# Byte places of the activations, and of both weight rings, in a two-layer decoder trunk

## The chip, the cores and the metric

One core of a Trainium2 chip runs the whole kernel. The metric is device time in microseconds of one launch, where lower is better. TensorE is called PE in the profile, VectorE DVE, ScalarE ACT, GpSimd POOL, and SP is the engine that issues most DMAs.

## What is computed

Sixteen learned meta tokens are put before 256 tokens of width 1024, and 272 tokens go through two layers of three sublayers each: a half-step feed-forward, a token mixer, a half-step feed-forward. Each has a norm before and one after it.

```python
h = concat([meta, x])                       # 272 x 1024, float32
for i in range(2):
    h += 0.5 * rms_norm(swiglu(rms_norm(h, g[0]), w_gate[i,0], w_up[i,0], w_down[i,0]), g[1])
    h += rms_norm(mixer(rms_norm(h, g[2])), g[3])     # i=0: retention and gated delta heads; i=1: window and stick-breaking heads
    h += 0.5 * rms_norm(swiglu(rms_norm(h, g[4]), w_gate[i,1], w_up[i,1], w_down[i,1]), g[5])
return h[16:]
# swiglu(x) = (silu(x @ w_gate) * (x @ w_up)) @ w_down, 1024 -> 2816 -> 1024
```

## The kernel before, in words

The activations lie transposed: 128 features on the partitions, eight blocks of them (`KD`, index kk) side by side, 272 tokens along a row. The weights come from memory in chunks of 128 partitions x 8 blocks x 256 columns of float32 (`RAW` = 2048 elements, 8192 bytes a partition; chunks of a down projection have 7 or 8 blocks). There are about 170 chunks, numbered n through the whole program.

*Splitting.* Each float32 value is split into a high part, rounded to the type float32r, and a low part, the rest, also float32r. A product is then three matmuls in float32r: high weights by high activations, low weights by high activations, high weights by low activations. That is `tile`: L1800, L1801, L1802, once for each of eight kk and each of the two 128-column halves of a chunk, 48 matmuls in all. In each of them the weights are the stationary operand (128x128) and the activations the moving one (272 columns, 256 where the meta tokens are no longer wanted). In the last down projection (`last_down`, L1888 to L1890) it is the other way: the weights move, 512 columns at a time, and the hidden activations are stationary. `first_tiles` (L1834, L1837, L1838), `half_tile` (L1872) and `out_half` (L2030) do the same products in other orders.

*Rings.* SP loads chunk n into slot n % 6 of `raw` (`NR` = 6). ScalarE (`hi`, L717) rounds it into slot n % 4 of `w_hi` (`NW` = 4), and VectorE (`lo`, L1179) writes the difference back over the same bytes, under the name `w_lo`. PE waits for the low part and reads both. Semaphores order the engines; `hi` and `lo` stand in each engine's program one to three chunks ahead of PE's use.

*Activations.* `u` (the sublayer's input) and `hid` (the hidden layer of a feed-forward) each have a high half and a low half. A row of them has `ROW` = 320 elements (1280 bytes) for 272 tokens, so that each kk begins at the same byte address modulo 256. Where the tokens start in a row is set by a number of bytes for each sublayer (`U_AT` for six sublayers, `HID_AT` for four feed-forwards). In "ab" the first half of the output projection reads two other buffers, `mix_hi` and `mix_lo`, whose rows are 1088 bytes. The six sublayers are, in order, ffn, ab, ffn, ffn, cd, ffn. The output projection of "cd" and the last sublayer skip the meta tokens and so begin 64 bytes later in a row.

*Places.* The address of a buffer modulo 256 follows from the assertion that `u_room` is at 64 and from the sizes: `raw` starts 49152 + 32768 + 1088 + 2176 = 85184 bytes before it, which is 192 modulo 256, so it starts at 128. All slots of `raw`, `w_lo` and `w_hi` are at 128 then, since a slot is 8192 bytes; a kk step in a chunk is 1024 bytes and the second half of its columns 512 bytes on, both nothing modulo 256. High and low `u` and `hid` are at 64, in the last feed-forward at 128 (and 192 with the skipped tokens). The scales of the norms, `gains`, sit in spare columns of `u`'s rows (elements 288 to 319), as do a few small tables of the "ab" mixer.

```python
def parts(name, rows_, where, shift):
    both = at(name, [P, 2 * rows_ * ROW], F32R, where)[:, :].rearrange("p (z k c) -> p z k c", z=2, c=ROW)
    cols = slice(shift // 4, shift // 4 + T)
    return both[:, 0, :, cols], both[:, 1, :, cols]
```

Of the kernel before, what the change touches and what calls it, by code (L numbers as in the profile page):

```python
# [22 lines left out]
F32 = mybir.dt.float32  # L23
# [5 lines left out]
P = 128  # L29
# [21 lines left out]
PLACE = 64  # L51
U_AT = (0, 0, 0, 0, 0, 64)
HID_AT = (0, 0, 0, 64)
# [99 lines left out]
def build(nc, a, c, out):  # L153
# [18 lines left out]
    with ctx:  # L172

        ring = place[0]
        raw = sb("raw", [NR, RAW])
        w_lo = at("w_lo", [P, NR, RAW], F32R, ring)
        w_hi = sb("w_hi", [NW, RAW], F32R)
        ss = sb("ss", [T])
        rstd = sb("rstd", [2, T])
        u_place = place[0]  # L180
# [28 lines left out]
        y_sq = at("y_sq", [P, 2, 2, T], F32, scratch)  # L209
        h_tok = at("h_tok", [P, 2, D], F32, place[0])  # L210
# [368 lines left out]
        def _(sp):  # L579
# [3 lines left out]
            def load(n, src, cols=CB):  # L583
# [3 lines left out]
                dst = raw[:, n % NR, 0:rows(n) * CB].rearrange("p (k c) -> p k c", c=cols)  # L587
                sp.dma_start(dst, src).then_inc(s_raw[n % NR], 16)

            for k, (kind, b, layer, f) in enumerate(subs):  # L590
                if kind == "ffn":
# [3 lines left out]
                    for j in range(NPAIR - 1):  # L595
                        if k == 0 and j == 0:
                            for k0, done in ((0, s_rawa), (KD // 2, s_raw[0])):
                                sp.dma_start(raw[:, 0, k0 * CB:(k0 + KD // 2) * CB].rearrange("p (k c) -> p k c", c=CB),
# [108 lines left out]
        def _(act):  # L707
            step = Steps(act, s_act)

            def hi(n):  # L710
# [6 lines left out]
                act.activation(w_hi[:, n % NW, 0:rows(n) * CB], raw[:, n % NR, 0:rows(n) * CB], ACT.Copy)\  # L717
# [46 lines left out]
            def pre_norm(k, kind, layer, b):  # L764
# [5 lines left out]
                for g in range(KD // 2):  # L770
                    if k == 0 and g == 2:
                        act.wait_ge(s_raw[0], 16)
                        act.activation(w_hi[:, 0, RAW // 2:RAW], raw[:, 0, RAW // 2:RAW], ACT.Copy).then_inc(s_hi, 1)
# [11 lines left out]
                if k == 0:  # L785
                    act.wait_ge(s_raw[1], 16)
                    for part, done in ((slice(0, RAW // 2), s_hia), (slice(RAW // 2, RAW), s_hi)):
                        act.activation(w_hi[:, 1, part], raw[:, 1, part], ACT.Copy).then_inc(done, 1)
# [345 lines left out]
            act.activation(w_hi[:, 0, 0:RAW // 2], raw[:, 0, 0:RAW // 2], ACT.Copy).then_inc(s_hia, 1)  # L1134
# [33 lines left out]
        def _(dve):  # L1168
# [4 lines left out]
            def lo(n):  # L1173
# [4 lines left out]
                src, dst = raw[:, n % NR, 0:rows(n) * CB], w_lo[:, n % NR, 0:rows(n) * CB]  # L1178
# [58 lines left out]
            def make_input(k, kind, layer):  # L1237
# [6 lines left out]
                for g in range(KD // 2):  # L1244
                    if k and g + 1 < KD // 2:
                        update_h(k, 2 * g + 2, 2 * g + 4)
                    if k == 0 and g == 2:
                        dve.wait_ge(s_hi, 1)
                        dve.tensor_tensor(w_lo[:, 0, RAW // 2:RAW], raw[:, 0, RAW // 2:RAW],
                                          w_hi[:, 0, RAW // 2:RAW].bitcast(F32), ALU.subtract).then_inc(s_lo, 1)  # L1250
                    input_lo(k, layer, g)
                if k == 0:
                    for part, ready, n, done in ((slice(0, RAW // 2), s_hia, 2, s_loa), (slice(RAW // 2, RAW), s_hi, 2, s_lo)):
                        dve.wait_ge(ready, n)
                        dve.tensor_tensor(w_lo[:, 1, part], raw[:, 1, part], w_hi[:, 1, part].bitcast(F32), ALU.subtract)\
# [1210 lines left out]
```

## Time and profile before

| | |
|---|---|
| median of 2 runs | 1092.18 us (1091.97 to 1092.39) |
| the profiled execution | 1091.99 us, of which the span of instructions is 1090.2 us |
| PE busy in the span | 1077.6 us, 8599 instructions |
| DVE busy | 703.7 us, 770 instructions |
| ACT busy | 545.4 us, 635 instructions |
| PE clock granted | 0.999 of full speed on the mean |
| memory traffic | 180.02 MB by DMA, mean 165 GB/s |

The page gives, for each engine, the time in which some instruction of it is under way. PE's matmuls overlap: a second one starts while the first is still in flight, so their durations add up to more than the busy time, and the distance from start to start is what the engine needs for one. Instructions of one line of the source are one group, and a group may mix shapes ("+1 forms"). A stretch of the timeline gives each instruction's start and duration; consecutive ones of one kind may be merged into one row with their count ("x2"). A window counts what overlaps it, so what was in flight at its left edge is counted too.

### The profile page before, as it was taken

Reading aid. Unit: us, or ns where it says so; the run is one execution under the profiler, and the core shown is the slowest. Engines: PE = TensorE matmul, PEld = TensorE weight load, DVE = VectorE, ACT = ScalarE, POOL = GpSimd, SP = SyncE. Lnnn points to the kernel's source line nnn. Section 1 sums busy time; section 2 is a strip of 40 time slices with the busy share of each in tenths; the row PEclk is TensorE's granted clock in tenths of the full one; section 3 lists DMA queues with packets and bytes.
Section 4 is the critical chain, followed back from the end, with each engine's and each line's share of the span. In section 5 each row is a group of like instructions: output and inputs, shape, how many; then the busy total and the mean of one; then the engine's idle time right before and its main releaser. Section 6 shows DMA issues by size and latency. Waiting matters only on the chain.

```text
span 1090.2 us, 19370 instructions
## 1 busy us (share of the span) xinstructions
PE 1077.6 (99%) x8599; PEld 1046.3 (96%) x8599; DVE 703.7 (65%) x770; ACT 545.4 (50%) x635; POOL 1.6 (0%) x13
## 2 busy tenths in 40 slices
PE   9999999999999999999999999999999999999997
PEld 8999999999999999999999999999999899999986
DVE  6755654588996777655546755654568867665552
ACT  5644343477564755343544644343575766444431
POOL 0000000000000000000000000000000000000000
PEclk9999999999999999999999999999999999999999
DMA  9666556857841455554554655555553245666451
GB/s 315 195 191 184 181 174 166 161 110 189 171 147 39 155 155 179 169 193 151 178 180 130 213 185 164 183 174 179 160 179 117 78 155 156 193 193 207 142 173 39
DMA packets 173073, 180.02 MB, mean 165 GB/s; under 512 B 7509, under 2 KB 165805, under 8 KB 172989
## 3 DMA queue, kind: packets, MB, share of 16 engines
q1 hardware_dynamic: 172668, 177.66, 54.0%
q8 instruction: 68, 1.11, 0.4%
q10 hardware_dynamic: 320, 1.11, 0.3%
q14 instruction: 17, 0.13, 0.0%
HBM read 177.05 MB, written 1.71 MB: 164 GB/s over the span
## 4 chain that ended last, share of the span: by engine, by line
PE 90%; DVE 6%; ACT 2%; issue 1%; DMA 1%; ACTq 0%; DVEq 0%
PE ps L1800 24%; PE ps L1802 23%; PE ps L1801 23%; PE ps L1905 5%; PE ps L1888 2%; PE ps L1890 2%; PE ps L1889 2%; PE ps L2030 2%; PE ps L1872 2%; PE ps L1834 1%; PE ps L1837 1%; PE ps L1838 1%; DVE hT L1228 1%; DVE w_lo L1179 1%; DVE yT L1227 1%
## 5 line engine op out<-in xcount | busy, mean ns | idle before, releaser
L1800 PE MATMUL ps<-u,w_hi 128*128 128x272 f32 (+1 forms) x1648 | 473.6, 287 | 1.2 <-DVE w_lo L1179 0.9
L1802 PE MATMUL ps<-u,w_hi 128*128 128x272 f32 (+1 forms) x1648 | 470.0, 285 | 0.0
L1801 PE MATMUL ps<-u,w_lo 128*128 128x272 f32 (+1 forms) x1648 | 469.7, 285 | 0.0
L1179 DVE TENSOR_TENSOR w_lo<-raw,w_hi 128x2048 fp32r<-128x2048 f32 (+2 forms) x167 | 369.5, 2237 | 106.0 <-ACT w_hi L717 105.9
L717 ACT ACTIVATE w_hi<-raw 128x2048 fp32r<-128x2048 f32 (+2 forms) x167 | 310.8, 1871 | 161.8 <-PE ps L1802 140.0
L1800 PEld LDWEIGHTS ps<-u,w_hi 128*128 128x128 f32 x1648 | 310.1, 188 | 3.3 <-issue 1.3
L1801 PEld LDWEIGHTS ps<-u,w_lo 128*128 128x128 f32 x1648 | 310.5, 188 | 0.3
L1802 PEld LDWEIGHTS ps<-u,w_hi 128*128 128x128 f32 x1648 | 310.4, 188 | 0.0
L1800 PE MATMUL ps<-hid,w_hi 128*128 128x272 f32 x528 | 151.3, 286 | 0.0
L1801 PE MATMUL ps<-hid,w_lo 128*128 128x272 f32 x528 | 151.3, 286 | 0.0
L1802 PE MATMUL ps<-hid,w_hi 128*128 128x272 f32 x528 | 151.3, 286 | 0.0
L1197 DVE TENSOR_TENSOR prod<-gates,ps 128x544 f32<-128x544 f32 (+1 forms) x44 | 31.4, 713 | 159.4 <-PE ps L1802 154.8
L724 ACT ACTIVATE gates<-gates 128x544 f32<-128x544 f32 (+1 forms) x44 | 28.8, 655 | 154.8 <-DVE gates L1187 154.7
L1801 PEld LDWEIGHTS ps<-hid,w_lo 128*128 128x128 f32 x528 | 99.4, 188 | 0.0
L1802 PEld LDWEIGHTS ps<-hid,w_hi 128*128 128x128 f32 x528 | 99.4, 188 | 0.0
L1800 PEld LDWEIGHTS ps<-hid,w_hi 128*128 128x128 f32 x528 | 99.4, 188 | 0.0
L1837 PE MATMUL ps<-u,w_hi 128*128 128x272 f32 (+1 forms) x160 | 40.9, 291 | 2.8 <-ACT u L781 2.4
L1187 DVE TENSOR_TENSOR gates<-ps,rstd 128x544 f32<-128x544 f32 (+1 forms) x44 | 31.4, 714 | 15.0 <-ACT rstd L757 13.3
L1838 PE MATMUL ps<-u,w_lo 128*128 128x272 f32 (+1 forms) x160 | 39.9, 285 | 0.0
L730 ACT ACTIVATE hid<-prod 128x544 fp32r<-128x544 f32 (+1 forms) x44 | 28.0, 637 | 23.7 <-DVE prod L1198 23.7
L1888 PE MATMUL ps<-w_hi,hid 128*128 128x512 f32 x88 | 34.8, 395 | 0.0
L1889 PE MATMUL ps<-w_lo,hid 128*128 128x512 f32 x88 | 34.7, 394 | 0.0
(345 smaller groups left out, 1046.4 us busy)
## 6 DMA issues: line engine op xcount, KB each, us to landing
raw<-ffn_w_up SPq DMA_DIRECT2D x44, 1024.0 KB, 5.4
raw<-ffn_w_gate SPq DMA_DIRECT2D x43, 1024.0 KB, 5.3
raw<-ffn_w_down SPq DMA_DIRECT2D x24, 896.0 KB, 4.8
raw<-ffn_w_down SPq DMA_DIRECT2D x20, 1024.0 KB, 5.1
raw<-ab_w_in SPq DMA_DIRECT2D x16, 1024.0 KB, 14.1
raw<-cd_w_in SPq DMA_DIRECT2D x9, 1024.0 KB, 5.3
raw<-ab_w_out SPq DMA_DIRECT2D x4, 1024.0 KB, 6.0
raw<-cd_w_out SPq DMA_DIRECT2D x4, 1024.0 KB, 5.1
```

The source lines that it names most:

```text
L717: act.activation(w_hi[:, n % NW, 0:rows(n) * CB], raw[:, n % NR, 0:rows(n) * CB], ACT.Copy)\
L1179: dve.tensor_tensor(dst, src, w_hi[:, n % NW, 0:rows(n) * CB].bitcast(F32), ALU.subtract)\
L1187: dve.tensor_tensor(gates[:, j % 2, :, tok], two(pair_banks(j), tok), rstd_two(1, tok), ALU.mult)\
L1197: step.done(dve.tensor_tensor(to, gates[:, j % 2, :, tok], two(pair_banks(j) + 2, tok), ALU.mult))
L1800: pe.matmul(o, wh, rhs_hi[:, kk, tok], start=first and kk == 0, stop=False)
L1801: pe.matmul(o, wl, rhs_hi[:, kk, tok], start=False, stop=False)
L1802: ins = pe.matmul(o, wh, rhs_lo[:, kk, tok], start=False, stop=last and kk == rows(n) - 1)
L1837: pe.matmul(o, wh, u_hi[:, kk, tok], start=kk == 0, stop=False, skip_group_check=True)
L1838: pe.matmul(o, wl, u_hi[:, kk, tok], start=False, stop=False, skip_group_check=True)
L1888: pe.matmul(o, hid_hi[:, kk, tok], wh, start=kk == 0, stop=False, skip_group_check=True)
L1889: pe.matmul(o, hid_hi[:, kk, tok], wl, start=False, stop=False, skip_group_check=True)
L1905: return pe.matmul(o, lhsT, rhs, start=start, stop=stop, skip_group_check=True)
```

## The change

Four things are done. The high and the low half of `u` and `hid` get a shift each, where they had one together. The slots of `raw` and `w_lo` become six buffers of their own with 0, 64, 192, 256, 384 and 448 bytes of extra distance from the ring's start, and a slot of `w_hi` becomes 64 bytes longer. The bases of `u` and `hid` go from 64 to 0 modulo 256. `gains` gets a buffer of its own, since a low half shifted by 128 bytes covers its old columns, and `lnv` moves into scratch space. In `out_half` the flag that marks the end of an accumulation is set at another matmul of the last three.

With the ring still starting at 128, the places are now: `w_lo` slots 128, 192, 64, 128, 0, 64; `w_hi` slots 64, 128, 192, 0; `u` high and low by sublayer as `U_AT` has them (64 more in "cd"'s output projection and in the last sublayer); `hid` as `HID_AT` has them; `mix_hi` and `mix_lo` begin at 192 (64 before), with their 1088-byte rows as before. The order of instructions and their waits are on every engine what they were.

```diff
-PLACE = 64
-U_AT = (0, 0, 0, 0, 0, 64)
-HID_AT = (0, 0, 0, 64)
+PLACE = 0
+SLOT = RAW + 16
+RAW_AT = (0, 16, 48, 64, 96, 112)
+U_AT = ((0, 64), (64, 0), (0, 128), (64, 128), (64, 64), (0, 128))
+HID_AT = ((64, 192), (0, 192), (32, 32), (0, 64))
...
         ring = place[0]
-        raw = sb("raw", [NR, RAW])
-        w_lo = at("w_lo", [P, NR, RAW], F32R, ring)
-        w_hi = sb("w_hi", [NW, RAW], F32R)
+        raw = [at(f"raw_{i}", [P, RAW], F32, ring + (i * RAW + far) * 4) for i, far in enumerate(RAW_AT)]
+        w_lo = [at(f"w_lo_{i}", [P, RAW], F32R, ring + (i * RAW + far) * 4) for i, far in enumerate(RAW_AT)]
+        place[0] += (NR * RAW + RAW_AT[-1]) * 4
+        w_hi = sb("w_hi", [NW, SLOT], F32R)
         ss = sb("ss", [T])
         rstd = sb("rstd", [2, T])
+        gains = sb("gains", [3, 4 * KD])
+        place[0] += (PLACE - place[0]) % 256
         u_place = place[0]
...
-        def parts(name, rows_, where, shift):
+        def parts(name, rows_, where, shifts):
 
             both = at(name, [P, 2 * rows_ * ROW], F32R, where)[:, :].rearrange("p (z k c) -> p z k c", z=2, c=ROW)
-            cols = slice(shift // 4, shift // 4 + T)
-            return both[:, 0, :, cols], both[:, 1, :, cols]
+            return [both[:, z, :, shift // 4:shift // 4 + T] for z, shift in enumerate(shifts)]
...
-        lnv = sb("lnv", [T])
...
-        w_ba, gains = spare[:, 0:KD, :], spare[:, KD:KD + 3, :]
+        w_ba = spare[:, 0:KD, :]
...
+        lnv = at("lnv", [P, T], F32, scratch + (HG + 1) * TP * 4)
...
-                src, dst = raw[:, n % NR, 0:rows(n) * CB], w_lo[:, n % NR, 0:rows(n) * CB]
+                src, dst = raw[n % NR][:, 0:rows(n) * CB], w_lo[n % NR][:, 0:rows(n) * CB]
...
-                    wh, wl = w_hi[:, n % NW, w], w_lo[:, n % NR, w]
+                    wh, wl = w_hi[:, n % NW, w], w_lo[n % NR][:, w]
...
-                                            stop=kk == KD - 1 and w_ is wl, skip_group_check=True)
+                                            stop=kk == KD - 1 and u_ is u_lo, skip_group_check=True)
...
-            dve.tensor_copy(gains, ps[:, 0, 0:12 * KD].rearrange("p (r c) -> p r c", c=32)).then_inc(s_gains, 1)
+            dve.tensor_copy(gains[:, :, :], ps[:, 0, 0:12 * KD].rearrange("p (r c) -> p r c", c=32)).then_inc(s_gains, 1)
```

The other lines of the diff only write the ring as a list (`raw[n % NR]`) in the DMAs and in the split of the first two chunks.

## Rows read from the trace of the kernel before

**Rows 1.** The page: its head and the busy time of each engine.

```profile
span 1090.2 us, 19370 instructions
PE 1077.6 (99%) x8599; PEld 1046.3 (96%) x8599; DVE 703.7 (65%) x770; ACT 545.4 (50%) x635; POOL 1.6 (0%) x13
```

**Rows 2.** The page: the chain that ended last, by engine and line.

```profile
PE 90%; DVE 6%; ACT 2%; issue 1%; DMA 1%; ACTq 0%; DVEq 0%
PE ps L1800 24%; PE ps L1802 23%; PE ps L1801 23%; PE ps L1905 5%; PE ps L1888 2%; PE ps L1890 2%; PE ps L1889 2%; PE ps L2030 2%; PE ps L1872 2%; PE ps L1834 1%; PE ps L1837 1%; PE ps L1838 1%; DVE hT L1228 1%; DVE w_lo L1179 1%; DVE yT L1227 1%
```

**Rows 3.** The waits of PE: total us, times, longest us.

```profile
PE ps L1837 <- ACT u L781: 2.4, 6, 0.5
PE ps L2377 <- POOL ones L685: 1.0, 1, 1.0
```

**Rows 4.** The window from 400 to 500 us, in the third sublayer.

```profile
core 0: us, PE busy (x) PEld busy (x) DVE busy (x) ACT busy (x) POOL busy (x), PEclk, DMA share, GB/s
400.00:500.00 100.00, 100.00 (x813) 100.00 (x812) 65.60 (x55) 47.80 (x41) 0.00 (x0) 1.00 0.58 185
```

**Rows 5.** The timeline of PE in the first feed-forward, 272 columns.

```profile
start us, us, engine line op out<-in xcount [idle before <-releaser]
99.76 0.28 PE L1802 MATMUL ps<-u,w_hi 128*128 128x272 f32 x1
99.88 0.29 PE L1800 MATMUL ps<-u,w_hi 128*128 128x272 f32 x1
...
100.99 0.28 PE L1800 MATMUL ps<-u,w_hi 128*128 128x272 f32 x1
```

**Rows 6.** The timeline of PE in "cd"'s output projection, 256 columns.

```profile
869.79 0.40 PE L1872 MATMUL ps<-u,w_hi 128*128 128x256 f32 x2
870.03 0.28 PE L1872 MATMUL ps<-u,w_lo 128*128 128x256 f32 x1
870.15 0.40 PE L1872 MATMUL ps<-u,w_hi 128*128 128x256 f32 x2
870.39 0.28 PE L1872 MATMUL ps<-u,w_lo 128*128 128x256 f32 x1
...
870.87 0.28 PE L1872 MATMUL ps<-u,w_hi 128*128 128x256 f32 x1
```

**Rows 7.** The timeline of PE in the last feed-forward, 256 columns.

```profile
949.83 0.28 PE L1800 MATMUL ps<-u,w_hi 128*128 128x256 f32 x1
...
950.89 0.28 PE L1800 MATMUL ps<-u,w_hi 128*128 128x256 f32 x1
```

**Rows 8.** The timeline of PE in "ab"'s output projection, rotating places.

```profile
356.27 0.29 PE L2030 MATMUL ps<-mix_hi,w_hi 128*128 128x272 f32 x1
356.40 0.29 PE L2030 MATMUL ps<-mix_lo,w_hi 128*128 128x272 f32 x1
356.53 0.29 PE L2030 MATMUL ps<-mix_hi,w_lo 128*128 128x272 f32 x1
...
357.41 0.29 PE L2030 MATMUL ps<-mix_hi,w_hi 128*128 128x272 f32 x1
```

**Rows 9.** Eight plain float32 matmuls of 272 columns: timeline and group.

```profile
244.46 1.99 PE L1905 MATMUL ps<-l2sq,ones 128*128 128x272 f32 x8
L1905 PE MATMUL ps<-l2sq,ones x8: 390/392/393, 244.5 to 246.1; 128*128 128x272 f32 x8
```

**Rows 10.** The timeline of PE in the last down projection, 512 columns.

```profile
1039.75 0.39 PE L1888 MATMUL ps<-w_hi,hid 128*128 128x512 f32 x1
...
1041.15 0.39 PE L1888 MATMUL ps<-w_hi,hid 128*128 128x512 f32 x1
```

**Rows 11.** The page: the two groups that split the chunks.

```profile
L1179 DVE TENSOR_TENSOR w_lo<-raw,w_hi 128x2048 fp32r<-128x2048 f32 (+2 forms) x167 | 369.5, 2237 | 106.0 <-ACT w_hi L717 105.9
L717 ACT ACTIVATE w_hi<-raw 128x2048 fp32r<-128x2048 f32 (+2 forms) x167 | 310.8, 1871 | 161.8 <-PE ps L1802 140.0
```

**Rows 12.** The page: DMA issues of one kind, us to landing.

```profile
raw<-ffn_w_gate SPq DMA_DIRECT2D x43, 1024.0 KB, 5.3
```

More of the change, by code:

```diff
@@ L586, in load @@
                     sp.wait_ge(s_used, n - NR + 1)
-                dst = raw[:, n % NR, 0:rows(n) * CB].rearrange("p (k c) -> p k c", c=cols)
+                dst = raw[n % NR][:, 0:rows(n) * CB].rearrange("p (k c) -> p k c", c=cols)
                 sp.dma_start(dst, src).then_inc(s_raw[n % NR], 16)
@@ L597, in _ @@
                             for k0, done in ((0, s_rawa), (KD // 2, s_raw[0])):
-                                sp.dma_start(raw[:, 0, k0 * CB:(k0 + KD // 2) * CB].rearrange("p (k c) -> p k c", c=CB),
+                                sp.dma_start(raw[0][:, k0 * CB:(k0 + KD // 2) * CB].rearrange("p (k c) -> p k c", c=CB),
                                              wg[:, k0:k0 + KD // 2, 0:CB]).then_inc(done, 16)
@@ L716, in hi @@
                     act.wait_ge(s_used, n - NW + 1)
-                act.activation(w_hi[:, n % NW, 0:rows(n) * CB], raw[:, n % NR, 0:rows(n) * CB], ACT.Copy)\
+                act.activation(w_hi[:, n % NW, 0:rows(n) * CB], raw[n % NR][:, 0:rows(n) * CB], ACT.Copy)\
                     .then_inc(s_hi, 1)
@@ L772, in pre_norm @@
                         act.wait_ge(s_raw[0], 16)
-                        act.activation(w_hi[:, 0, RAW // 2:RAW], raw[:, 0, RAW // 2:RAW], ACT.Copy).then_inc(s_hi, 1)
+                        act.activation(w_hi[:, 0, RAW // 2:RAW], raw[0][:, RAW // 2:RAW], ACT.Copy).then_inc(s_hi, 1)
                     for m in (2 * g, 2 * g + 1):
@@ L787, in pre_norm @@
                     for part, done in ((slice(0, RAW // 2), s_hia), (slice(RAW // 2, RAW), s_hi)):
-                        act.activation(w_hi[:, 1, part], raw[:, 1, part], ACT.Copy).then_inc(done, 1)
+                        act.activation(w_hi[:, 1, part], raw[1][:, part], ACT.Copy).then_inc(done, 1)
                     hi(2)
@@ L1133, in _ @@
             act.wait_ge(s_rawa, 16)
-            act.activation(w_hi[:, 0, 0:RAW // 2], raw[:, 0, 0:RAW // 2], ACT.Copy).then_inc(s_hia, 1)
+            act.activation(w_hi[:, 0, 0:RAW // 2], raw[0][:, 0:RAW // 2], ACT.Copy).then_inc(s_hia, 1)
             act.wait_ge(s_gains, 1)
@@ L1248, in make_input @@
                         dve.wait_ge(s_hi, 1)
-                        dve.tensor_tensor(w_lo[:, 0, RAW // 2:RAW], raw[:, 0, RAW // 2:RAW],
+                        dve.tensor_tensor(w_lo[0][:, RAW // 2:RAW], raw[0][:, RAW // 2:RAW],
                                           w_hi[:, 0, RAW // 2:RAW].bitcast(F32), ALU.subtract).then_inc(s_lo, 1)
@@ L1254, in make_input @@
                         dve.wait_ge(ready, n)
-                        dve.tensor_tensor(w_lo[:, 1, part], raw[:, 1, part], w_hi[:, 1, part].bitcast(F32), ALU.subtract)\
+                        dve.tensor_tensor(w_lo[1][:, part], raw[1][:, part], w_hi[:, 1, part].bitcast(F32), ALU.subtract)\
                             .then_inc(done, 1)
@@ L1742, in _ @@
             dve.wait_ge(s_hia, 1)
-            dve.tensor_tensor(w_lo[:, 0, 0:RAW // 2], raw[:, 0, 0:RAW // 2], w_hi[:, 0, 0:RAW // 2].bitcast(F32), ALU.subtract)\
+            dve.tensor_tensor(w_lo[0][:, 0:RAW // 2], raw[0][:, 0:RAW // 2], w_hi[:, 0, 0:RAW // 2].bitcast(F32), ALU.subtract)\
                 .then_inc(s_loa, 1)
@@ L1830, in first_tiles @@
                                     w = slice(kk * CB + m * P, kk * CB + m * P + P)
-                                    wh, wl = w_hi[:, (n + z) % NW, w], w_lo[:, (n + z) % NR, w]
+                                    wh, wl = w_hi[:, (n + z) % NW, w], w_lo[(n + z) % NR][:, w]
                                     o = ps[:, bank + 2 * z + m, tok]
@@ L1869, in half_tile @@
                     w = slice(kk * CB + m * P, kk * CB + m * P + P)
-                    wh, wl = w_hi[:, n % NW, w], w_lo[:, n % NR, w]
+                    wh, wl = w_hi[:, n % NW, w], w_lo[n % NR][:, w]
                     for w_, u_ in ((wh, u_hi), (wl, u_hi), (wh, u_lo)):
@@ L1886, in last_down @@
                                 w = slice((kk - k0) * BANK, (kk - k0 + 1) * BANK)
-                                wh, wl = w_hi[:, n % NW, w], w_lo[:, n % NR, w]
+                                wh, wl = w_hi[:, n % NW, w], w_lo[n % NR][:, w]
                                 pe.matmul(o, hid_hi[:, kk, tok], wh, start=kk == 0, stop=False, skip_group_check=True)
@@ L2027, in out_half @@
                         w = slice(kk * CB + m * P, kk * CB + m * P + P)
-                        wh, wl = w_hi[:, n % NW, w], w_lo[:, n % NR, w]
+                        wh, wl = w_hi[:, n % NW, w], w_lo[n % NR][:, w]
                         for w_, u_ in ((wh, uh), (wh, ul), (wl, uh)):
                             ins = pe.matmul(ps[:, bank, 0:T], w_, u_[:, kk, :], start=kk == 0 and w_ is wh and u_ is uh,
-                                            stop=kk == KD - 1 and w_ is wl, skip_group_check=True)
+                                            stop=kk == KD - 1 and u_ is u_lo, skip_group_check=True)
                     return ins
@@ L2382, in first_chunk @@
                     pe.wait_ge(s_lo, 1) if g else pe.wait_ge(s_hia, 1)
-                    for part, (u_, w_) in enumerate(((u_hi, w_hi), (u_hi, w_lo), (u_lo, w_hi))):
+                    for part, (u_, w_) in enumerate(((u_hi, w_hi[:, 0, :]), (u_hi, w_lo[0]), (u_lo, w_hi[:, 0, :]))):
                         if part == 1 and g == 0:
@@ L2390, in first_chunk @@
                                 w = slice(kk * CB + m * P, kk * CB + m * P + P)
-                                ins = pe.matmul(ps[:, 4 + m, :T], w_[:, 0, w], u_[:, kk, :], start=part == 0 and kk == 0,
+                                ins = pe.matmul(ps[:, 4 + m, :T], w_[:, w], u_[:, kk, :], start=part == 0 and kk == 0,
                                                 stop=part == 2 and kk == KD - 1, skip_group_check=True)
```

## The prediction

> **What bounds the kernel now.** I read the page first. TensorE is busy 1077.6 of 1090.2 us, VectorE 703.7, ScalarE 545.4 [rows 1], and the chain that ended last runs 90% on TensorE, most of it on the three lines of `tile` (L1800, L1801, L1802) [rows 2]. So the reader is to see one engine that hardly pauses. The list of waits confirms it: its longest entry in total is 2.4 us [rows 3]. In the middle of a feed-forward sublayer, from 400 to 500 us, TensorE is busy the whole 100 us, VectorE 65.6, ScalarE 47.8, and the granted clock is 1.00 of 2.4 GHz [rows 4]. No other engine is near to being the bound there, so only the distance from the start of one matmul to the start of the next (the pitch) sets the time. A matmul's own duration (about 285 ns) contains its flight through the array and overlaps its neighbours, so pitches must be read from starts.
>
> **The pitch, by where its operands stand.** I use "place" for an SBUF byte address modulo 256.
>
> - 272 columns (feed-forward), both activations at place 64, weights at 128: starts at 99.76 and ten matmuls later at 100.99, 123 ns [rows 5]; finer, 100 us with 813 matmuls, of which two were in flight at the window's left edge, is 100,000 / 811 = 123.3 ns [rows 4]. 272 columns at 2.4 GHz are 113.3 ns, so 10.0 ns are extra.
> - 256 columns, activations at place 128 (64 and the 16 skipped tokens), weights also at 128 (the output projection of the sublayer "cd"): 869.79 to 870.87, nine pitches, 120.0 ns [rows 6].
> - 256 columns, activations at 192, weights at 128 (last sublayer, the only one that is shifted before): 949.83 to 950.89, nine pitches, 117.8 ns [rows 7]. 64 bytes made 2.2 ns.
> - 272 columns with places that rotate, `mix_hi` and `mix_lo` (a row of them is 1088 bytes, so kk = 1, 2, 3 stand at 128, 192 and 0): 356.27 to 357.41, nine pitches, 126.7 ns [rows 8]. If the three at 192 take the 123.3 of the feed-forward, the six at 128 and 0 take (1140 - 370) / 6 = 128.3, 5.0 more.
> - The same 272 columns in plain float32, two instructions at two clocks a column: eight cover 1.99 us, the last of them 0.392, so seven pitches are 1.60 us, 228.5 ns each, against 226.7 by columns [rows 9]. Only about 2 ns are extra. So the 10.0 ns is no fixed price of a matmul: some 8 ns of it belong to streams that take one column per clock, and that part has been seen to depend on place.
> - 512 columns (the last down projection): 1039.75 to 1041.15, six pitches, 233.3 ns, 20.0 extra [rows 10].
>
> **The change part by part.** No instruction is added, removed or moved on any engine, and no wait changes: the queues hold the same list with other addresses. There are 7656 of these float32r matmuls: 6144 of 272 columns, 1248 of 256, 264 of 512.
>
> 1. *Low activations parted from the high ones.* `u` is parted in five of six sublayers, `hid` in two of the three whose moving operand it is. Counted by buffer that is u 1056 x 4 + 864 (with the second half of "ab"'s output projection) and hid 528 x 2, 6144 matmuls; `u` of "cd" (624), hid_2 (528) and `mix` (96) stay together. No row of before shows a low operand at another place than the high one. Bounds: at best the whole extra beyond the 2 ns of plain float32 goes, about 8 ns for 6144 of 272 columns (49 us), 9 for 1248 of 256 (11 us), 18 for 264 of 512 (5 us), 65 us in all. At worst each of 272 columns pays the 5.0 ns of the rotated places, 31 us, and each of 1056 of 256 columns 2.2 ns, 2 us, 33 us in all. I take the row nearest in kind, the one step of 64 bytes at equal shape: 2.2 ns for each parted matmul, 6144 x 2.2 = 13.5 us gained. The reason for the sign: before, every matmul of a stretch repeats one relation of moving stream, next weights and next stream, so whatever collides, collides in each; parting and uneven slots end that lockstep. That is my choice, not a measurement, and the weakest step here.
> 2. *Uneven ring slots, `u` and `hid` bases at 0.* `w_hi` slots now stand at 64, 128, 192, 0 and `w_lo` slots at 128, 192, 64, 128, 0, 64, so each distance between activation and weights occurs about equally often. By itself that could cost as the rotated places do; I put it with step 1 (its bounds are the same 33 us and 65 us), at nothing more, since the two act on the same reads. If the cover fails it is the third case below.
> 3. *ScalarE and VectorE on new places.* L717 (1871 ns, 167 times) and L1179 (2237 ns) [rows 11] write and read the slots. A chunk lasts 48 x 123.3 = 5.9 us on TensorE and these two engines are idle for half and a third of that [rows 4], so 100 ns either way per chunk is covered; without cover it would be 167 x 0.1 = 17 us.
> 4. *DMA rows of 1024 bytes to shifted slots.* A chunk lands 5.3 us after its issue [rows 12], the ring holds six chunks of 5.9 us, and the DMA engines are busy at 0.58 [rows 4]. Nothing; a landing late by 1 us would still be covered.
> 5. *`gains` as a buffer of its own, `lnv` in scratch, another stop flag in `out_half`.* One copy of 96 columns stays one copy. Nothing; at most tens of ns for six sublayers.
>
> Sum: 1092.0 (the profiled execution: span 1090.2 and 1.8 around it, 0.2 below the median of 1092.18) - 13.5 = 1078.5 us. All falls evenly on matmuls, so no wait takes its place: with a pitch of 121 ns a chunk is 5.8 us and VectorE's share rises from 66% to 67%.
>
> **Rivals.**
>
> *Nothing happens, 1092.* The shift that is known to work (2.2 ns) was of both activations against the weights, not of one against the other. If what counts is only the mean over many relations, the parting may give back what the slots take. For it: pitches in rows 5 stay at 123 whatever ScalarE and VectorE do, so reads don't compete with other engines. Against it: rows 6, 7 and 8 show three different extras. In the Trainium skill, "SBUF — State Buffer", section "Who interferes with whom", TensorE's moving operand and its weights have a read port each and only VectorE's and GpSimd's shared pair causes contention; by that rule no place matters and the time stays. The trace disagrees as far as rows 6 and 7 go, 120.0 against 117.8 ns at one shape. The same skill, "TensorE: Matmul & The Clock Gate", section "Back-to-back issue gap", gives N/2.4 + 2.5 ns as the gap of a lone warm matmul, 115.8 ns for 272 columns, an estimate from that page; rows 5 show 123.3.
>
> *Slower, 1108.* One mechanism: a matmul is dear when its moving operand's place less that of the weights loaded while it runs is 0 or 128 (their distance, modulo 256). The rows say so at both shapes: distance 0 costs 2.2 ns (256 columns), 0 and 128 cost 5.0 (272 columns). Before, practically all 272-column matmuls stand at distance 192, a cheap one. After, four evenly spread `w_hi` slots put half of all matmuls at a dear distance, whatever the activations' places are. 3072 x 5.0 = 15.4 us, and 528 x 2.2 = 1.2 us in the last sublayer, less 0.2 that "cd"'s output projection gains: 1092.0 + 16.4 = 1108. It decides wherever the distance to the weights matters more than the distance between low and high. Against it: its 5.0 ns rest on nine pitches, in a stretch where both the place and the step between successive operands change, and I cannot tell these apart.
>
> *Much faster, 1060.* Half of the 65 us goes, if the collisions are between the end of one stream and the start of the next, and both parts of the change thin them. Nothing in the rows measures it.
>
> **How the numbers follow.** A gain near 1079: 0.42, with a range of its own from 1066 to 1088. No change (1088 to 1096): 0.23. Slower, 1096 to 1120: 0.29. Much faster: 0.06. Measurement of this kernel can tell about 2% from no change. Faster by more than that, below 1070.3, holds the last case and a part of the first: 0.20. Slower, above 1114, is the upper end of the third: 0.09. Within: 0.71. The range for 8 in 10 is 1065 to 1109.
>
> **What would show it.** Right: in the profile after, pitches near 121 ns in the feed-forward stages, shorter in those with parted activations than in "cd"'s input projection and in the third down projection, which keep theirs together, and TensorE as busy as before. Slower case: pitches that change with the chunk, every second `w_hi` slot dear, near 128. No change: 123.3 everywhere. My sum is wrong altogether if TensorE's waits grow beyond some 6 us, or if the pitch of the hid stage with both at 32 falls as far as the parted ones.

## The result, and the profile after

The changed kernel takes 1103.74 us (1103.11 to 1104.37, 2 runs) against 1092.18: 1.0096 times as long, 95% interval 1.0074 to 1.0118. It is 11.6 us slower. The forecast was 1078.5; the time lies inside the forecast range and on the wrong side of no change.

The page of the changed kernel, head and busy times, with the chain of the same page (the lines of the matmuls and of the splitting stand four further down in the file):

```profile
span 1101.3 us, 19370 instructions
PE 1088.8 (99%) x8599; PEld 1058.4 (96%) x8599; DVE 703.8 (64%) x770; ACT 545.2 (50%) x635; POOL 1.6 (0%) x13
...
PE 93%; DVE 3%; ACT 2%; issue 1%; DMA 1%; ACTq 0%; DVEq 0%
...
L1183 DVE TENSOR_TENSOR w_lo<-raw,w_hi 128x2048 fp32r<-128x2048 f32 (+2 forms) x167 | 369.5, 2236 | 108.0 <-ACT w_hi L721 108.0
L721 ACT ACTIVATE w_hi<-raw 128x2048 fp32r<-128x2048 f32 (+2 forms) x167 | 310.7, 1870 | 167.8 <-PE ps L1806 145.9
```

Against [rows 1, 2, 11]: the span has grown by 11.1 us and TensorE's busy time by 11.2. TensorE has 93% of the chain that ended last, for 90%. VectorE, ScalarE, the bytes moved and the two splitting groups (2236 and 1870 ns for 2237 and 1871) are as they were. The waits of TensorE on the activations are as short as before [rows 3]:

```profile
PE ps L1841 <- ACT u L785: 2.2, 5, 0.5
```

So nearly all of the loss is in the pitch. TensorE in three windows of the changed kernel (us, busy with count, granted clock, DMA share, GB/s):

```profile
core 0: us, PE busy (x), PEclk, DMA share, GB/s
60.00:140.00 80.00, 80.00 (x639) 1.00 0.57 176
400.00:500.00 100.00, 100.00 (x799) 1.00 0.58 182
884.00:902.00 18.00, 18.00 (x156) 1.00 0.52 163
```

The granted clock is 1.00 of 2.4 GHz and no time is idle, but from 400 to 500 us there are 799 matmuls for 813 before [rows 4]. Less the two in flight at the edge, that is 125.5 ns for 123.3. The last window is "cd"'s output projection, 256 columns: 156 for the 152 of a window of 18 us there before, 116.9 for 120.0 ns. The timeline of TensorE in the changed kernel at 272, 256 and 512 columns:

```profile
99.94 0.29 PE L1804 MATMUL ps<-u,w_hi 128*128 128x272 f32 x1
...
101.08 0.29 PE L1804 MATMUL ps<-u,w_hi 128*128 128x272 f32 x1
...
881.82 0.28 PE L1876 MATMUL ps<-u,w_lo 128*128 128x256 f32 x1
...
883.22 0.28 PE L1876 MATMUL ps<-u,w_lo 128*128 128x256 f32 x1
...
1049.79 0.39 PE L1892 MATMUL ps<-w_hi,hid 128*128 128x512 f32 x1
...
1051.18 0.39 PE L1892 MATMUL ps<-w_hi,hid 128*128 128x512 f32 x1
```

These are 126.7 ns (nine pitches; 123 in [rows 5]), 116.7 (twelve; 120.0 in [rows 6]) and 231.7 (six; 233.3 in [rows 10]). A single chunk says little here, since the pitch changes from chunk to chunk. The table has the mean over each whole stage, from the starts of groups of three matmuls without a wait between them. The columns "even slots" and "together" are the two experiments that each undo one half of the change.

| stage | matmuls | before | after | even slots | together |
|---|---|---|---|---|---|
| u, 1st sublayer | 1056 | 123.33 | 125.80 | 126.58 | 125.41 |
| hid, 1st | 528 | 123.33 | 124.93 | 124.44 | 125.86 |
| u, "ab" | 864 | 123.4 | 125.70 | 124.98 | 125.45 |
| u, 3rd | 1056 | 123.33 | 125.31 | 124.49 | 125.63 |
| hid, 3rd | 528 | 123.33 | 125.86 | 125.92 | 125.56 |
| u, 4th | 1056 | 123.33 | 125.54 | 124.45 | 125.66 |
| hid, 4th | 528 | 123.33 | 125.33 | 123.34 | 125.52 |
| u, "cd", in | 432 | 123.38 | 125.2 | 123.37 | 125.2 |
| u, "cd", out, 256 columns | 192 | 120.0 | 116.6 | 120.0 | 116.6 |
| u, last, 256 columns | 1056 | 117.78 | 117.88 | 117.76 | 117.57 |
| last down, 512 columns | 264 | 233.34 | 231.53 | 228.98 | 231.82 |

The differences times the counts are 13.0 us in the eight rows of 272 columns, and -0.7, +0.1 and -0.5 us in the last three: 12.0 us, where the span grew by 11.1. Most of the remainder is in "ab", whose stages took 170.5 us from first to last matmul for 169.3, 1.2 us more where its pitches make 2.0: waits there take up part of it.

### The profile page after: what moved, and what is told of

Read it like the earlier page. It is cut to its first block, busy times and chain, and to the rows that moved or that the text cites. A ratio compares the mean times of both kernels' runs of the same rounds, so it can differ in the third digit from the quotient of the medians.

```text
span 1101.3 us, 19370 instructions
## 1 busy us (share of the span) xinstructions
PE 1088.8 (99%) x8599; PEld 1058.4 (96%) x8599; DVE 703.8 (64%) x770; ACT 545.2 (50%) x635; POOL 1.6 (0%) x13
## 4 chain that ended last, share of the span: by engine, by line
PE 93%; DVE 3%; ACT 2%; issue 1%; DMA 1%; ACTq 0%; DVEq 0%
PE ps L1804 24%; PE ps L1805 24%; PE ps L1806 24%; PE ps L1909 6%; PE ps L1893 2%; PE ps L1892 2%; PE ps L1894 2%; PE ps L2034 2%; PE ps L1876 1%; PE ps L1838 1%; PE ps L1841 1%; PE ps L1842 1%; DVE hT L1232 1%; DVE yT L1231 1%; DMA x_tok<-meta_tokens 1%
## 5 line engine op out<-in xcount | busy, mean ns | idle before, releaser
L1183 DVE TENSOR_TENSOR w_lo<-raw,w_hi 128x2048 fp32r<-128x2048 f32 (+2 forms) x167 | 369.5, 2236 | 108.0 <-ACT w_hi L721 108.0
L721 ACT ACTIVATE w_hi<-raw 128x2048 fp32r<-128x2048 f32 (+2 forms) x167 | 310.7, 1870 | 167.8 <-PE ps L1806 145.9
```

Of the source, the lines that this page charges most:

```text
L721: act.activation(w_hi[:, n % NW, 0:rows(n) * CB], raw[n % NR][:, 0:rows(n) * CB], ACT.Copy)\
L1183: dve.tensor_tensor(dst, src, w_hi[:, n % NW, 0:rows(n) * CB].bitcast(F32), ALU.subtract)\
```

## The experiments

All are the changed kernel with small edits. None leaves out any part of the computation. Ratios are against the kernel before on the same chip. "Distance" is the place of the moving operand less the place of the weights, modulo 256; before it is 192 for 272 columns (outside `mix`), with low and high together. A pair such as (0, 64) gives the places of the high and of the low activations.

### Even slots, parted activations

```diff
-SLOT = RAW + 16
-RAW_AT = (0, 16, 48, 64, 96, 112)
+SLOT = RAW
+RAW_AT = (0, 0, 0, 0, 0, 0)
```

> The changed kernel with all slots of both rings back at place 128 (activations as changed). 'Distance' theory (a matmul is dear when its moving operand's place less that of the weights loaded meanwhile is 0 or 128, some 128.3 ns against 123.3 at 272 columns): pitches of 126.6 in u of the first sublayer (0, 64), 125.0 in ab (64, 0), 128.3 in the third (0, 128), 125.0 in the fourth (64, 128), 123.3 in cd (64, 64), 123.3 in hid 0 (64, 192), 126.6 in hid 1 (0, 192); together about 15 us over before, 1107. 'Step' theory (dear when the next moving operand begins 0 or 128 after the end of the last one): 126.6 where low and high are 64 apart and in hid 1, 123.3 elsewhere, the third sublayer included; about 1104. 'Slots' theory (the uneven slots cost all, parting gains 2.2 ns a matmul as forecast): 1078.5.

1099.69 us, ratio 1.0073 [1.0058, 1.0088]. Slower, so parting alone costs, with even slots. Its windows in the first and the third sublayer:

```profile
60.00:140.00 80.00, 80.00 (x634) 1.00 0.57 176
400.00:500.00 100.00, 100.00 (x804) 1.00 0.57 179
```

126.6 and 124.7 ns. None of the three theories fits. The third sublayer, (0, 128), has both halves at distances that the distance theory calls dear; it was to take 128.3 by that theory and 123.3 by the step theory, and took 124.45. No parted stage of 272 columns is below 123.33; the two that stay together are still there (the table, hid in the 4th and "cd"). By the table, pitches times counts make 8.0 us, of a measured 7.5. hid in the 4th has both halves at 32, which is distance 160, and takes 123.34: as much as at distance 192.

### Uneven slots, activations together

```diff
-U_AT = ((0, 64), (64, 0), (0, 128), (64, 128), (64, 64), (0, 128))
-HID_AT = ((64, 192), (0, 192), (32, 32), (0, 64))
+U_AT = ((64, 64), (64, 64), (64, 64), (64, 64), (64, 64), (128, 128))
+HID_AT = ((64, 64), (64, 64), (64, 64), (128, 128))
```

> The changed kernel with the activations back together at the places of before (64; 128 in the last feed-forward and sublayer), slots uneven. Distance: half of all matmuls at a dear distance, pitch near 125.8 in every stage of 272 columns, about 1108. Step: the steps are those of before (192 everywhere), so 123.3 and 1092. Slots (parting had gained 13.5): the parting's gain is lost on top of 1103.7, about 1117.

1103.24 us, 1.0100 [1.0083, 1.0117]: the slots alone cost as much as the whole change. The two halves don't add up (7.5 + 11.05 = 18.6 us, measured 11.6). By the table every stage of 272 columns is near 125.5 ns with uneven slots, wherever its activations stand, so with the slots uneven the parting has little left to cost. The step theory (1092) and the slots theory (1117) are refuted; the distance theory's 125.8 is near. Five starts of chunks of this run's first sublayer, TensorE's timeline:

```profile
66.16 0.29 PE L1804 MATMUL ps<-u,w_hi 128*128 128x272 f32 x1
...
72.08 0.29 PE L1804 MATMUL ps<-u,w_hi 128*128 128x272 f32 x1
...
78.16 0.29 PE L1804 MATMUL ps<-u,w_hi 128*128 128x272 f32 x1
...
108.41 0.28 PE L1804 MATMUL ps<-u,w_hi 128*128 128x272 f32 x1
...
114.28 0.29 PE L1804 MATMUL ps<-u,w_hi 128*128 128x272 f32 x1
```

With 48 matmuls a chunk, the first takes 123.3 ns a matmul (`w_hi` and `w_lo` both at 128), the next 126.7 (192 and 0) and the one from 108.41 on 122.3 (64 and 0). Twelve pairs of ring places take turns, and only two of them have both rings at one place.

### Only the slots of `w_hi` uneven

```diff
-RAW_AT = (0, 16, 48, 64, 96, 112)
+RAW_AT = (0, 0, 0, 0, 0, 0)
```

together with the activations of the run before.

> Activations together as before, w_lo slots all at 128, only the w_hi slots at 128, 192, 0, 64. Distance: two of three matmuls run while high weights load, half of these at a dear distance: pitch 123.3 + 5.0/3 = 125.0, about 1102. Within one chunk: 123.3 with w_hi at 128 or 0, 126.6 with w_hi at 192 or 64. Step: 1092. A theory that only the change of place between successive weights is dear (123.3 where w_hi and w_lo are both at 128, more in the three other slots): about 1101 with three of four chunks dear.

1097.42 us, 1.0049 [1.0034, 1.0064]. Four chunks in a row, TensorE's timeline, the first matmul of each and of the next:

```profile
447.67 0.29 PE L1804 MATMUL ps<-u,w_hi 128*128 128x272 f32 x1
...
453.60 0.29 PE L1804 MATMUL ps<-u,w_hi 128*128 128x272 f32 x1
...
459.68 0.29 PE L1804 MATMUL ps<-u,w_hi 128*128 128x272 f32 x1
...
465.70 0.28 PE L1804 MATMUL ps<-u,w_hi 128*128 128x272 f32 x1
...
471.57 0.29 PE L1804 MATMUL ps<-u,w_hi 128*128 128x272 f32 x1
```

48 matmuls each: 5.93, 6.08, 6.02 and 5.87 us, or 123.5, 126.7, 125.4 and 122.3 ns with `w_hi` at 128, 192, 0 and 64. The pitch follows the slot, but not as the distance theory had it, which expected `w_hi` at 0 to be cheap and at 64 dear. The last chunk is cheaper than before's, which led to two of the runs below.

### Only the slots of `w_lo` uneven

```diff
-SLOT = RAW + 16
+SLOT = RAW
-        place[0] += (NR * RAW + RAW_AT[-1]) * 4
+        place[0] += (NR * RAW + RAW_AT[-1] + 16) * 4
```

also with the activations together; the second line keeps `w_hi` at 128.

> Activations together as before, w_hi slots even at 128, only the w_lo slots at 128, 192, 64, 128, 0, 64. Uneven w_hi slots alone gave 1097.4, both rings uneven 1103.2, before 1092.2. If the two rings cost separately and add up: 1098. If what counts is only that no single set of places repeats, one uneven ring is as bad as two: 1103. Chunks with w_lo at 128 should stay at 123.3.

1100.99 us, 1.0073 [1.0058, 1.0088]. By the place of `w_lo`: 123.4 at 128, 125.3 at 0, 125.5 at 64, 126.6 at 192. Three of four places are dear here, where for `w_hi` it was two of four. By medians, each against the kernel before on its own chip, `w_hi`'s slots cost 5.2 us, `w_lo`'s 8.4, both 11.05: less than the sum of 13.6.

### A map of pairs, even slots

```diff
+U_AT = ((0, 0), (0, 64), (192, 192), (128, 0), (192, 0), (0, 0))
+HID_AT = ((128, 128), (192, 64), (128, 64), (64, 0))
```

> A map: slots even at 128, each stage of 272 columns with another pair of places (high, low) of its activations. Distance: u first sublayer (0, 0) 128.3; hid 0 (128, 128) 128.3; ab (0, 64) 126.6; third sublayer u (192, 192) 123.3; hid 1 (192, 64) 123.3; fourth u (128, 0) 128.3; hid 2 (128, 64) 126.6; cd (192, 0) 125.0. Step: (0, 0), (128, 128), (192, 192), (192, 64) and (128, 0) 123.3; (0, 64), (128, 64) and (192, 0) 126.6. Last sublayer, 256 columns, both at 64 (distance 192, step 0): by distance 117.8 as in rows 7. The whole near 1112 by distance, 1098 by step.

One execution: 1098.38 us. The 1098 of the step theory is met by luck: its pitches are not, (0, 0) was to take 123.3 and took 126.66. Each stage tries a pair, so the profile is a map. Its windows in the first, third and last sublayer:

```profile
60.00:140.00 80.00, 80.00 (x633) 1.00 0.57 176
400.00:500.00 100.00, 100.00 (x790) 1.00 0.57 179
910.00:1028.00 118.00, 118.00 (x1042) 1.00 0.60 190
```

Stage means of this run, of "even slots" and of before taken together, 272 columns, all weights at 128, by (high, low):

| together | ns | parted | ns |
|---|---|---|---|
| (64, 64), distance 192 | 123.33 | (64, 128), (64, 192), (192, 64), (128, 64), (128, 0), (0, 128) | 124.44 to 124.49 |
| (128, 128), distance 0 | 125.32 | (192, 0) | 125.05 (124.6 without its first two chunks) |
| (0, 0), distance 128 | 126.66 | (64, 0) | 124.98 |
| (192, 192), distance 64 | 126.67 | (0, 192) | 125.92 |
| | | (0, 64), in two stages | 126.58 and 125.58 |

Fourteen of sixteen pairs were run, and the one of before is the cheapest. The right half is not dear throughout: eight of the ten parted pairs are below the 125.3 to 126.7 of the three other pairs together, and (0, 128) at 124.45 is 2.2 ns under (0, 0). So parting costs from distance 192 and mostly gains from the others, and a parted pair is not the mean of what its two distances cost together. "ab" and the first chunks of a sublayer run their products in other orders, which may be why (0, 64) has two pitches. At 256 columns the order is another: 120.0 at distance 0 and 117.8 at 64 before [rows 6, 7], and 113.3 here at 192 (118,000 / 1040 = 113.5 in the window).

### Only the low halves parted

```diff
-PLACE = 0
+PLACE = 64
+U_AT = ((0, 64), (0, 64), (0, 64), (0, 64), (0, 64), (64, 64))
+HID_AT = ((0, 64), (0, 64), (0, 64), (64, 64))
```

with even slots: every high half where it was before, the low halves of the first five sublayers 64 bytes on. This is the cleanest trial of step 1.

> The prediction's first step alone: everything as before (even slots at 128, high activations at 64, the last sublayer and feed-forward untouched), only the low activations of the first five sublayers and three feed-forwards at 128. The prediction's step: 2.2 ns less for each parted matmul, 1079. Its opposite, after the two maps: the pair (64, 64) is the cheapest of the fourteen measured at 272 columns and (64, 128) costs 124.45 instead of 123.33, so about 6000 x 1.1 = 6.7 us more, 1099.

1097.99 us (1097.77 to 1101.73, 4 runs), 1.0064 [1.0046, 1.0081]; 124.44 to 124.55 ns in all eight stages of 272 columns:

```profile
60.00:140.00 80.00, 80.00 (x645) 1.00 0.58 179
400.00:500.00 100.00, 100.00 (x804) 1.00 0.59 188
877.00:895.00 18.00, 18.00 (x156) 1.00 0.44 135
```

Parting costs 1.1 ns for each matmul of 272 columns, 6.8 us for 6048 of them, one third of the step from distance 192 to the dearest places. The last window is "cd"'s output projection, 256 columns, whose high half stands at distance 0: there the same parting gains 2.2 ns, 117.8 for 120.0, which is 0.4 us for 192 matmuls. Together 6.4 us; measured are 5.7 by the medians and 7.0 by the ratio.

### Everything 64 bytes on

```diff
-PLACE = 0
+PLACE = 128
-        ring = place[0]
+        ring = place[0] = place[0] + 64
+U_AT = ((0, 0), (0, 0), (0, 0), (0, 0), (0, 0), (64, 64))
+HID_AT = ((0, 0), (0, 0), (0, 0), (64, 64))
```

with even slots: both rings at 192, activations at 128, so all distances are those of before.

> Everything as before but 64 bytes on: rings at 192, activations at 128 (0 in the last sublayer), hid likewise. If only the distance between activations and weights counts, every stage of 272 columns is at 123.3 and the time is 1092, as before. If the absolute place counts, 125 to 127 in some or all stages, 1103 to 1110. It also carries the gains buffer, lnv in scratch and the other stop flag of the change: 1092 clears them.

1092.41 us (10 runs), 0.9999 [0.9989, 1.0009]. TensorE's windows in the third and the last sublayer and in the last down projection:

```profile
400.00:500.00 100.00, 100.00 (x811) 1.00 0.59 185
905.00:1015.00 110.00, 110.00 (x935) 1.00 0.62 197
1024.00:1080.00 56.00, 56.00 (x250) 1.00 0.34 115
```

Stage means are 123.33, 117.78 and 233.34, before's own. So moving everything by 64 bytes changes nothing; it is the relation between activations and weights that counts, and not the place. This kernel still holds the separate `gains`, the moved `lnv` and the other stop flag, so these cost nothing that can be measured (within 0.1%).

### The last sublayer at distance 192

```diff
+U_AT = ((64, 64), (64, 64), (64, 64), (64, 64), (64, 64), (0, 0))
+HID_AT = ((64, 64), (64, 64), (64, 64), (0, 64))
```

with even slots at 128. The stationary hidden activations of the last down projection move with it, to 64 and 128 in place of 192.

> Even slots at 128 and activations at 64 as before, except that the moving operand of the last sublayer (256 columns) stands at 64 instead of 192, and the stationary hidden activations of the last down projection at 64 (high) and 128 (low) instead of 192. If the pitch belongs to the pair of places alone, the stretches seen in the first four runs carry over: 113.3 for 256 columns in the last sublayer (1056 matmuls x 4.5 = 4.7 us) and 229.0 for 512 (264 x 4.3 = 1.1 us): 1086.4, under both kernels. If the 113.3 belonged to the other arrangement around it, 1092.

1088.02 us (1086.34 to 1090.52, 6 runs), 0.9953 [0.9938, 0.9968]: faster than both kernels. TensorE's timeline in the last sublayer, its window there, and a window of all engines in "ab", of this run and of the kernel before:

```profile
949.75 0.28 PE L1804 MATMUL ps<-u,w_hi 128*128 128x256 f32 x1
...
951.11 0.28 PE L1804 MATMUL ps<-u,w_hi 128*128 128x256 f32 x1
```

```profile
905.00:1015.00 110.00, 110.00 (x967) 1.00 0.61 197
...
260.00:310.00 50.00, 48.09 (x386) 46.95 (x385) 43.29 (x74) 27.69 (x31) 0.00 (x0) 0.97 0.72 162
...
260.00:310.00 50.00, 49.55 (x435) 48.09 (x428) 46.04 (x79) 28.09 (x35) 0.00 (x0) 1.00 0.70 170
```

Twelve pitches in 1.36 us are 113.3 ns. 1056 x (117.8 - 113.4) = 4.6 us, and 512 columns at 229.1 for 233.3 give 264 x 4.2 = 1.1: 5.7 in all, 1086.9 by this chip's 1092.6, which the two lowest runs reach (1086.34 and 1086.57). The profiled run was the longest (1090.52); in it the granted clock is 0.97 from 260 to 310 us, where the kernel before has 1.00, and "ab" is some 3.3 us longer. The clock fell behind a pause: TensorE waited 1.91 us for VectorE's `w_lo`, until 287.25, and the granted clock from 288 to 290 is 0.50 (1.2 GHz), with 227 ns for a matmul:

```profile
287.25 0.53 PE L1804 MATMUL ps<-u,w_hi 128*128 128x272 f32 x1 [1.91 <-DVE w_lo L1183]
...
288.00:290.00 2.00, 2.00 (x11) 2.00 (x10) 2.00 (x4) 2.00 (x3) 0.00 (x0) 0.50 0.17 52
```

The same trace holds one thing more, in the first chunks of the last sublayer, where nothing about the places changes:

```profile
903.00:912.00 9.00, 9.00 (x78) 1.00 0.01 2
...
914.25 0.62 PE L1854 MATMUL ps<-h_sq,ones 128*128 128x272 f32 x2
...
914.60:923.60 9.00, 9.00 (x81) 1.00 0.92 300
```

The pitch is 118.4 ns until 914.25 (78 less two in 9 us), where two plain float32 matmuls of the norm stand in the stream, and 113.3 in all chunks behind them. The last 24 before them run in the order of those behind. The run below, with the same places in this sublayer, has 113.3 in front of them too.

### The same, with "cd"'s output projection at distance 192 too

```diff
+        o_hi, o_lo = parts("u_out", KD, u_place, (0, 0))
...
-                    tiles(n + i, 2 * block_at("cd", i), u_hi, u_lo, final=i == 3, tok=out_tokens(k))
+                    tiles(n + i, 2 * block_at("cd", i), o_hi, o_lo, final=i == 3, tok=out_tokens(k))
```

and the same names where these activations are written.

> The kernel with the last sublayer at 64, and in addition the mixed activations of cd's output projection (256 columns) written and read at 64 instead of 128. 192 matmuls from 120.0 to 113.3: 1.3 us under that kernel's 1088.0, 1086.7. It tells whether 113.3 goes with distance 192 at 256 columns wherever in the program it is.

1086.80 us (1086.12 to 1090.4, 5 runs), 0.9953 [0.9941, 0.9966]. The projection falls from 120.0 to 113.3 ns:

```profile
872.00:890.00 18.00, 18.00 (x162) 1.00 0.45 142
...
899.70:908.70 9.00, 9.00 (x81) 1.00 0.01 2
```

The step is seen in the trace (192 x 6.7 = 1.3 us), but the two kernels' times can't be told apart. The second window is the start of the last sublayer: 81 matmuls in 9 us where the run before has 78.

### The ring of `w_hi` at 64

```diff
-        place[0] += (NR * RAW + RAW_AT[-1]) * 4
+        place[0] += (NR * RAW + 48) * 4
```

added to "the last sublayer at distance 192", so that every chunk has the relation that was 122.3 ns in one chunk of four.

> As the kernel with the last sublayer at 64, and in addition the whole w_hi ring at 64 with w_lo at 128. If the 122.6 of the chunks with w_hi at 64 in the run with uneven w_hi slots is a property of that set of places: 272 columns 122.6, 6144 x 0.7 = 4.3 us under 1086.4 if the 256 and 512 columns stay, 1082. If it was carried from chunk to chunk (a chunk starts in the state the one before left), the pitch is nearer to the 126.4 that the same distances gave with both rings uneven: up to 19 us more, 1105.

1109.20 us, 1.0147 [1.0130, 1.0164], the slowest of all, and beyond the 1105 of its expectation. Its window in the third sublayer:

```profile
400.00:500.00 100.00, 100.00 (x791) 1.00 0.57 179
```

126.66 ns in every feed-forward stage of 272 columns, all with `w_hi` and activations at 64 and `w_lo` at 128, as in the chunk that took 122.3. The cheap chunk did not carry over.

### `w_hi` at 192, `w_lo` at 128, activations at 192

```diff
-PLACE = 0
+PLACE = 192
-        place[0] += (NR * RAW + RAW_AT[-1]) * 4
+        place[0] += (NR * RAW + 16) * 4
+U_AT = ((0, 0), (0, 0), (0, 0), (0, 0), (0, 0), (192, 64))
+HID_AT = ((0, 0), (0, 0), (0, 0), (128, 192))
```

> Even slots, w_hi at 192 and w_lo at 128, activations at 192 (so high weights and activations share a place and w_lo is 64 below): the set at which single chunks ran at 122.2 ns in the run with the activations together and both rings uneven. If that rhythm holds when every chunk has this set: 272 columns 122.2, 6144 x 1.1 = 6.9 us less than before; last sublayer (high at 192, low at 64) 115.6 as single chunks had, 2.3 us less; 1083. If, as in the run with the w_hi ring at 64, a set of places has a second, slower rhythm and is never tipped out of it: 125 to 127, 1102 to 1112.

1101.97 us, 1.0085 [1.0071, 1.0099]: 125.77 ns at 272 columns. The other relation that was cheap in single chunks (122.3 ns from 108.41 on in "together", whose places are these less 128) is dear in a long stretch; only 256 columns came as foreseen, at 115.6.

### Three of four `w_hi` slots at 64

```diff
+    AT = (0, 16, 16, 16)
...
+        k0 = n * RAW + self.AT[n]
```

with even `w_lo` slots, the `w_hi` ring starting at 0, activations together at 64 and the last sublayer at distance 192. It asks whether the cheap rhythm needs an entry from another place.

> w_lo at 128, activations at 64, the four w_hi slots at 0, 64, 64, 64. With w_hi at 64 two pitches have been seen at the same places: 122.2 in the chunks that followed one with w_hi at 0, and 126.6 when every chunk was at 64. If the entry decides and the rhythm is kept: the three chunks after each chunk at 0 all at 122.2, that one at 125.5, mean 123.0. If the rhythm lasts only one chunk: 122.2, then 126.6 twice, mean 125.2. If something else than the entry made the difference: 126.6 in all three.

1103.10 us, 1.0097 [1.0082, 1.0113]. TensorE's timeline in the first and in the third sublayer, both in chunks with `w_hi` at 64 and the same activation places:

```profile
60.05 0.29 PE L1818 MATMUL ps<-u,w_hi 128*128 128x272 f32 x1
...
61.93 0.29 PE L1818 MATMUL ps<-u,w_hi 128*128 128x272 f32 x1
...
439.88 0.28 PE L1818 MATMUL ps<-u,w_hi 128*128 128x272 f32 x1
...
441.71 0.28 PE L1818 MATMUL ps<-u,w_hi 128*128 128x272 f32 x1
```

```profile
400.00:500.00 100.00, 100.00 (x812) 1.00 0.58 181
600.00:700.00 100.00, 100.00 (x793) 1.00 0.56 179
```

Fifteen pitches take 1.88 us there, 125.3 ns, and 1.83 us here, 122.0. Over the chunks at 64 the means are 126.6 ns in the first and fourth sublayer and 122.23 in the third, while the chunks at 0 between them are 125.55 throughout. Of the three expectations the first holds for the third sublayer and the last for the others. So the same places have two rhythms, and each lasts for some hundreds of matmuls at least. It isn't tied to the whole sublayer: in the third sublayer the first two chunks are at 126.5 ns, in another order of the products, and 122 begins behind the norm's two plain float32 matmuls at 405.82, as the change to 113.3 in "the last sublayer at distance 192" does behind the same two. In the first and fourth sublayer they stand in the stream as well (26.59 and 605.39) and nothing changes. What decides was not found, and no run tried to steer it.

## Why the prediction was wrong, step by step

**The bound** was right. TensorE is busy throughout, its pitch alone sets the time, and 11.2 of the 11.6 us are TensorE's busy time.

**Step 1**, the low activations parted, -2.2 ns for each of 6144 matmuls, is the step that failed, in its sign. Its reason was that before "every matmul of a stretch repeats one relation of moving stream, next weights and next stream", so that whatever collides collides in each, and the parting ends that. What the runs show in its place: the relation that was repeated is the cheapest of the fourteen pairs measured, so there was nothing to escape from. With nothing but the low halves moved each matmul of 272 columns took 1.1 ns more; with this change's pairs and even slots the step costs 7.5 us, though 1056 of the 6144, the last sublayer's, stayed at 117.8. The idea itself is not empty: moving the low half did gain 2.2 ns, by 128 bytes from (0, 0) at 272 columns and by 64 bytes from distance 0 at 256. But the one row that varies the relation at 272 columns, [rows 8], was 3.4 ns dearer than the repeated one of [rows 5], and the prediction used it as a bound and not for the sign. The forecast's 2.2 ns were taken from two distances at 256 columns, 0 and 64 [rows 6, 7]. At 272 columns 64 is dearer than 0 (126.67 and 125.32), so even that row's sign does not hold at the other width. The guess about sign rested on a picture of collisions, not on a row.

**Step 2**, the uneven slots at nothing more, failed too: alone they cost 11.05 us, and with them in place the parting adds only the rest, 0.5, which the intervals don't tell from nothing. So the measured 11.6 us are the slots' before they are the parting's. A spread over relations leaves the cheapest one. The four distances with both rings at one place average (123.3 + 125.3 + 126.7 + 126.7) / 4 = 125.5 ns, and the stages show 125.2 to 125.86. That the two agree is no proof: ten of the twelve pairs of ring places in "together" have the rings at different places, and these go from 122.3 to 126.7. The bound of 33 us held.

**Steps 3, 4 and 5** held: the splitting groups are unchanged to a nanosecond, waits and DMA too, and the run with everything 64 bytes on puts `gains`, `lnv` and the flag at nothing (1.0 within 0.1%).

**The rivals.** "Nothing", 1092, is refuted: the same instructions took 113.3, 117.8 or 120.0 ns at 256 columns by where their operands stood. The Trainium skill, "SBUF — State Buffer", section "Who interferes with whom", gives TensorE's moving operand and its weights a read port each and says nothing of places; read as the prediction read it, both kernels take one time, and these traces disagree with that. "Slower", 1108, was the nearest by 4.3 us. What the runs bear out is its broad part, that the relation to the weights decides and that uneven slots cost whatever the activations do. Its rule for a single matmul (dear at distance 0 and 128, whatever its neighbours) fails: distance 64 is as dear as 128 with the halves together, and (0, 128), dear twice by the rule, took 124.45. That its total came near is partly luck: it had two dear distances of four by 5.0 ns, 2.5 on the mean; measured with even rings are three of four, by 2.0, 3.3 and 3.3, which is 2.1. The 5.0 came out of the rotating places [rows 8], where step and place are mixed, as the prediction warned, and where it gave the matmuls at place 192 the 123.3 ns that the feed-forward has at place 64; at 192 the map has 126.67. Its test, "pitches that change with the chunk", is seen in the `w_hi` run. It also missed a cost that exists without uneven slots, the parting itself from distance 192. The "much faster" case has nothing for it.

What stays open is the cause below the distances. No run shows which two accesses meet, why 256 and 272 columns rank the distances differently, or what picks the rhythm. Since one set of places can have two pitches, each pitch of the map is that of one or two stages, and not of the places for good; the 123.33 of before returned in every feed-forward stage of four traces.

## What to carry to other kernels

Where a stream of matmuls has no gaps left, place is a cost like any other: keep every slot of a ring at one byte distance from the moving operand, and choose that distance by measuring a whole stage at each. If the relation that repeats is a dear one, moving one of the halves may help; if it is the cheapest, every other place costs. One kernel can map some ten pairs, a pair for each stage, in one run, but the two rhythms ask for a second stage of each pair before it is trusted. Don't assume that variety helps, don't carry a distance from one column count to another, and don't carry a pitch from a single chunk of a mixed pattern to a uniform one: two such relations were 1 ns better in short stretches and 2.4 and 3.3 ns worse in uniform use. Before forecasting a sign, ask whether any row has the sign, or only the size.

## What the hardware showed that was not expected

- The float32r matmuls here take the same time when everything moves by 64 bytes, 0.9999 [0.9989, 1.0009], and up to 1.5% more over the kernel when activations and weights move against each other.
- At 272 columns moving the low half alone by 64 bytes costs 1.1 ns from distance 192; moving it by 128 gains 2.2 ns from (0, 0).
- At 256 columns the pitch is 120.0, 117.8 or 113.3 ns at distances 0, 64 and 192, up to 6% of such a matmul; used in the last sublayer it makes a kernel 0.5% faster than the one before.
- Two rhythms, 122.2 and 126.6 ns at 272 columns and 113.3 and 118.4 at 256, at the same places modulo 256 and a granted clock of 1.00. Twice the change from one to the other fell on two plain float32 matmuls in the stream.
- 123.33 ns is not the floor at 272 columns, yet no kernel here held less than it over all of its stages.
